# A fused two-block transformer on one core: weight splitting one tile further ahead among the gating steps of the second layer's FFN, and eighteen w_ada tiles moved into the first layer's FFN

## The chip, the core and the metric

The kernel runs on one core of a Trainium2 chip, as one program. The metric is the device time of one execution in microseconds (us). Five engines run their own instruction streams and meet at semaphores: TensorE (PE), VectorE (DVE), ScalarE (ACT), GpSimd (POOL) and SyncE (SP), which here only issues the DMAs.

## What is computed

A first block of two layers is followed by a second block of one layer. For this change, three pieces of the reference matter: the modulation vectors of each layer (`adaln_params`), the gated convolutional FFN, and the query projection of the second block's expert layer.

```python
def adaln_params(cvec, w_ada, b_ada):          # for c and for c_ctx
    m = jax.nn.silu(cvec) @ w_ada + b_ada      # w_ada: 1024 x 6144
    return jnp.split(m, 6, axis=-1)

def conv_ffn(h, w_up, conv_w, w_down):         # D_FF = 2816
    up = h @ w_up
    a, b = up[..., :D_FF], up[..., D_FF:]
    return (jax.nn.silu(dwconv3(a, conv_w)) * b) @ w_down

# trunk_layer, l = 0 (256 tokens and 256 context tokens) and l = 1 (256 tokens only):
x = x + gt1 * (mix @ w_out)
x = x + gt2 * conv_ffn(modulate(rmsnorm(x, g2), sh2, sc2), w_up, ffn_conv, w_down)

# second block: the same adaln, a mixer, then _peer, which begins with
q = (xb @ w_query).reshape(PEER_BLOCK, PEER_HEADS, 2, PEER_HALF)
```

## The kernel before

All weights stream from HBM in tiles of 128 x 1024 floats (512 KB), in one fixed order that `weight_tiles` writes down. Each tile lands in one of four buffers (`RAW`, `NRAW = 4`). SP issues the load of tile i when tile i-4 has been released, and it waits for that in the order of the list, so a late release holds back every later load.

A weight tile is not multiplied in one pass. ACT writes its rounded copy to `TH` ("high"), DVE or POOL writes the remainder to `TL` ("low"), and PE then runs three matmuls for each of the eight rows k (`mm3`: high x high, high x low, low x high). There are three such split buffers (`NSPLIT = 3`), so splitting tile j needs PE to be done with split tile j-3. A tile is released in `RAW` when its low part is written. `highs(n)` on ACT and `lows(n)` on DVE split, in order, every tile up to number n. `later(key, d)` is the split tile d places after `key`; `AHEAD = 2` is the usual distance.

The tiles of `w_ada` (48 for each of the three layers, 144 in all) are an exception: they are not split. PE multiplies them straight out of `RAW` with the silu of c in `SC`, into a bank of their own (`ada` on PE), and they occupy their `RAW` buffer until then. Every fourth one ends a group g: ACT copies the bank to `AROW`, and before the first tile of the next group PE turns that row into columns (`columns(g)`), to which DVE adds the bias. Groups in `ADA_TURNED` are turned at points written out by hand instead. `_ada_plan` says at which point of the program which w_ada tile stands: `("unit", l, u)` are points in attention, `("up", l, m)` and `("down", l, third, m)` points in the FFN, `("lstm", u)` and `("wq", m)` points in the second block.

The FFN of layer l has 22 gating steps m, in thirds of 8, 8 and 6. Step m projects tile `("wup", l, m)` (the part a), then tile `("wup", l, 22 + m)` (the part b). ACT copies a to `OC` times the middle tap (`conv_mid`), DVE adds the two outer taps, ACT applies silu, DVE multiplies by b ("gated"), ACT writes the rounded result to `MIDh` and DVE the remainder to `MIDl`. After each third come eight tiles `("wdn", l, third, i)` that multiply the mids, and DVE adds each result to X (`residual`). In the first layer a matmul row has 512 columns (48 matmuls of 256 columns for a tile), in the second 256 (24 matmuls for a tile). After the third third of the first layer, ACT squares each row of X for the next norm, and PE can go on only when that norm is done.

In the second layer's first third ACT also squares the context of the second block (`ctx`), and behind the first third PE sums it. Between the second layer's tiles wup 1 and wup 2, SP also loads a block of constants (`in_cs2`), for which it waits until the norm has read what lies there.

Where the splits stand among the gating steps of both layers, on ACT and on DVE:

```python
highs(later(("wup", l, mm_), 3 if mm_ == 0 else AHEAD))   # ACT, ahead of conv_mid
...
if mm_:
    highs(later(("wup", l, 22 + mm_), AHEAD))             # ACT, behind silu, ahead of MIDh
...
lows(later(("wup", l, mm_), 3 if mm_ == 0 else AHEAD))    # DVE, ahead of the taps
...
if mm_:
    lows(later(("wup", l, 22 + mm_), AHEAD))              # DVE, behind the taps, ahead of gated
```

## Time and profile before

| | us |
|---|---|
| median of three runs | 2350.66 (2347.52 to 2355.02) |
| the profiled execution, its own time | 2337.34 |
| its span, first to last instruction | 2335.6 |
| PE busy | 2172.3 (93%) |
| DVE busy | 1285.3 (55%) |
| ACT busy | 1086.5 (47%) |
| DMA, mean rate | 152 GB/s |
| mean granted clock of TensorE | 0.957 of full |

PE busy counts each matmul from its issue to its modelled end, and those overlap, so 93% does not mean that PE has little left to lose: a matmul of 256 columns has a duration of about 280 ns but the next may start 113 ns after it. The granted clock is 1 at 2.4 GHz and 0.5 at 1.2 GHz.

### The profile page before, as it was taken

The numbers are of one execution on the slowest core, as the hardware profiler recorded it, in microseconds if no ns is written. First come the engines' busy times: TensorE is split into PE (matmuls) and PEld (weight loads), VectorE is DVE, ScalarE is ACT, GpSimd is POOL, SyncE is SP. The second block draws the span as 40 slices with busy tenths as digits, with TensorE's granted clock in tenths as the row PEclk, the third lists the DMA queues.
The fourth block names the chain that finished last, engine by engine and source line by source line (L and its number), as shares of the span: only waits on it lengthen the run. The fifth ranks groups of instructions, "written<-read, shape, count | busy, mean of one in ns | idle before, by whom it ended". The sixth has DMA issues, their size and how long they took to land.

```text
span 2335.6 us, 44498 instructions
## 1 busy us (share of the span) xinstructions
PE 2172.3 (93%) x19132; PEld 2038.7 (87%) x19132; DVE 1285.3 (55%) x2517; ACT 1086.5 (47%) x1880; POOL 485.4 (21%) x230
## 2 busy tenths in 40 slices
PE   4989999999999888899878998899999999999998
PEld 3967889999999678888857888899999999999998
DVE  2253444343444465455546255559938898666665
ACT  3333343232235335344533344555567776655564
POOL 0201100000002110000211234128866665000000
PEclk8999989999998899999879999999999999999999
DMA  7224323434433245655323333465644444566654
GB/s 272 73 82 137 126 86 141 146 136 154 154 118 121 73 166 190 222 172 204 114 69 128 135 118 126 154 226 186 195 153 145 151 145 157 193 196 192 197 191 135
DMA packets 97284, 355.01 MB, mean 152 GB/s; under 512 B 10688, under 2 KB 11712, under 8 KB 96704
## 3 DMA queue, kind: packets, MB, share of 16 engines
q1 hardware_dynamic: 97088, 352.18, 44.8%
q8 instruction: 150, 2.46, 0.4%
q14 instruction: 46, 0.38, 0.0%
HBM read 351.09 MB, written 1.05 MB: 151 GB/s over the span
## 4 chain that ended last, share of the span: by engine, by line
PE 77%; DVE 8%; ACT 5%; issue 5%; DMA 4%; POOL 2%; SPq 0%; DVEq 0%; POOLq 0%; ACTq 0%
PE ps L79 72%; PE ps L84 4%; DVE TL L114 3%; ACT TH L158 3%; PE ps L107 1%; POOL TL L114 1%; DMA RAW<-in_wup 1%; DMA RAW<-in_wada 1%; DMA RAW<-in_wdn 1%; DVE l1oc L126 1%; POOL SM L114 1%; ACT SQ L155 1%; DMA RAW<-in_win 0%; ACT l1oc L155 0%; DMA RAW<-in_wq 0%
## 5 line engine op out<-in xcount | busy, mean ns | idle before, releaser
L158 ACT ACTIVATE TH<-RAW 128x1024 fp32r<-128x1024 f32 (+1 forms) x515 | 539.5, 1049 | 395.1 <-PE ps L79 155.8
L114 DVE TENSOR_TENSOR TL<-RAW,TH 128x1024 fp32r<-128x1024 f32 (+1 forms) x339 | 414.3, 1222 | 416.8 <-ACT TH L158 416.3
L114 POOL TENSOR_TENSOR TL<-RAW,TH 128x1024 fp32r<-128x1024 f32 x176 | 423.3, 2408 | 606.8 <-ACT TH L158 588.3
L79 PE MATMUL ps<-Hh,TL 128*128 128x256 f32 x1920 | 457.6, 291 | 52.5 <-POOL TL L114 19.0
L79 PE MATMUL ps<-Hh,TH 128*128 128x256 f32 x1920 | 444.8, 284 | 0.0
L79 PE MATMUL ps<-Hl,TH 128*128 128x256 f32 x1920 | 443.6, 284 | 0.0
L79 PEld LDWEIGHTS ps<-Hh,TL 128*128 128x128 f32 x1920 | 327.4, 195 | 84.8 <-issue 28.2
L79 PE MATMUL ps<-HXh,TL 128*128 128x256 f32 x1312 | 368.2, 285 | 17.4 <-DVE TL L114 12.0
L79 PE MATMUL ps<-HXh,TH 128*128 128x256 f32 x1312 | 361.8, 280 | 0.0
L79 PE MATMUL ps<-HXl,TH 128*128 128x256 f32 x1312 | 361.0, 279 | 0.0
L79 PE MATMUL ps<-W,TH 128*128 128x256 f32 x2048 | 348.2, 276 | 0.0
L79 PEld LDWEIGHTS ps<-Hh,TH 128*128 128x128 f32 x1920 | 327.8, 195 | 0.1
L79 PEld LDWEIGHTS ps<-Hl,TH 128*128 128x128 f32 x1920 | 327.7, 195 | 0.0
L79 PEld LDWEIGHTS ps<-W,TH 128*128 128x128 f32 x2048 | 308.6, 188 | 0.0
L79 PE MATMUL ps<-W,TL 128*128 128x256 f32 x1024 | 283.2, 277 | 1.5 <-DVE G L114 1.5
L79 PEld LDWEIGHTS ps<-HXh,TL 128*128 128x128 f32 x1312 | 248.2, 191 | 21.2 <-DVE TL L114 13.5
L79 PEld LDWEIGHTS ps<-HXh,TH 128*128 128x128 f32 x1312 | 248.4, 191 | 0.0
L79 PEld LDWEIGHTS ps<-HXl,TH 128*128 128x128 f32 x1312 | 247.4, 190 | 0.0
L79 PEld LDWEIGHTS ps<-W,TL 128*128 128x128 f32 x1024 | 192.3, 188 | 1.7 <-DVE G L114 1.7
L114 POOL TENSOR_TENSOR ACC<-SQ 128x512 f32<-128x512 f32 (+1 forms) x6 | 7.6, 1269 | 604.1 <-ACT SQ L155 604.1
L126 DVE SCALAR_TENSOR_TENSOR X<-ps,ADA,X 128x256 f32<-128x256 f32 x104 | 47.1, 480 | 136.3 <-PE ps L79 136.3
L155 ACT ACTIVATE W<-W,T 128x128 fp32r<-128x128 f32 x256 | 82.0, 391 | 64.6 <-DVE W L114 64.6
(323 smaller groups left out, 3070.2 us busy)
## 6 DMA issues: line engine op xcount, KB each, us to landing
RAW<-in_wada SPq DMA_DIRECT2D x144, 512.0 KB, 3.9
RAW<-in_ut SPq DMA_DIRECT2D x128, 512.0 KB, 3.5
RAW<-in_v SPq DMA_DIRECT2D x128, 512.0 KB, 3.5
RAW<-in_wup SPq DMA_DIRECT2D x88, 512.0 KB, 3.7
RAW<-in_win SPq DMA_DIRECT2D x74, 512.0 KB, 3.7
RAW<-in_wdn SPq DMA_DIRECT2D x32, 512.0 KB, 4.5
RAW<-in_wout SPq DMA_DIRECT2D x24, 512.0 KB, 3.6
RAW<-in_wq SPq DMA_DIRECT2D x16, 512.0 KB, 3.7
```

Source lines behind the costliest of these rows:

```text
L79: return self.e.matmul(out, lhs, rhs, start=first, stop=last, skip_group_check=skip)
L84: return self.e.matmul(out, lhs, rhs, start=first, stop=last, tile_position=at)
L107: return self.e.transpose(out, src, eye)
L114: return DRY if self.e is None else self.e.tensor_tensor(out, a, b, op)
L126: return self.e.scalar_tensor_tensor(out=out, in0=a, scalar=s, in1=b, op0=op0, op1=op1)
L155: return DRY if self.e is None else self.e.activation(out, a, fn, **kw)
L158: return DRY if self.e is None else self.e.activation(out, a, ACT.Copy, **kw)
```

## The change

1. In the second layer's FFN (l = 1), the splits among the gating steps run three tiles ahead instead of two, and they stand elsewhere: on ACT one behind `conv_mid` and one behind silu, on DVE one behind the taps and one behind the multiplication by b. The last of the eight wdn steps of the first and second thirds also splits three ahead.
2. Eighteen w_ada tiles move forward in the plan: eight leave the second layer's gating steps, two the lstm points and eight the wq points. Ten get a new point `"between"` (between a and b of the first layer's steps 12 to 21), eight stand at the wdn steps of the first layer's last third. All that follow shift along: the second layer's attention now holds tiles 0 to 9 of the third w_ada, for instance. Group 21, 23, 27 and 33 are now turned like the others.
3. SC gets the next layer's silu right behind the last tile of a w_ada on ACT, no longer ahead of the first tile of the next.
4. In the wdn steps of both layers DVE splits ahead of the residual, no longer behind it.

```diff
@@ weight_tiles
                 add(("wup", l, m), ins[f"wup{l}"][m])
+                ada("between", l, m)
                 add(("wup", l, 22 + m), ins[f"wup{l}"][22 + m])
...
         add(("wq", m), ins["wq2"][m])
-        ada("wq", m)
@@ _ada_plan
-    plan += [(("up", 0, m), 1) for m in range(8)]
-    plan += [(("down", 0, 0, m), 1) for m in range(8)]
-    plan += [(("up", 0, m), 1) for m in range(8, 16)]
-    plan += [(("down", 0, 1, m), 1) for m in range(8)]
-    plan += [(("up", 0, m), 1) for m in range(16, 22)]
+    for third in range(3):
+        for m in range(8 * third, min(8 * third + 8, 22)):
+            plan += [(("between", 0, m), 1)] * (m >= 12) + [(("up", 0, m), 1)]
+        plan += [(("down", 0, third, m), 1) for m in range(8)]
...
-    plan += [(("up", 1, m), 1) for m in range(8)]
...
-    plan += [(("lstm", u), 1) for u in range(6)]
-    plan += [(("wq", m), 1) for m in range(1, 16, 2)]
+    plan += [(("lstm", u), 1) for u in range(4)]
-ADA_TURNED = (3, 9, 11, 21, 23, 27, 33, 35)
+ADA_TURNED = (3, 9, 11, 35)
@@ scalar_program, ada
-                if i == 0 and b:
-                    act.wait_ge(P, *used("wada", b - 1, 47))
-                    act.act(SC, par(["c1", "c1", "c2"][b]), ACT.Silu).then_inc(*A.mark("sc", b))
...
+                if i == 47 and b < 2:
+                    act.act(SC, par(["c1", "c2"][b]), ACT.Silu).then_inc(*A.mark("sc", b + 1))
@@ scalar_program, gating steps
-                    highs(later(("wup", l, mm_), 3 if mm_ == 0 else AHEAD))
+                    if l == 0:
+                        highs(later(("wup", l, mm_), 3 if mm_ == 0 else AHEAD))
                     act.wait_ge(P, *used("wup", l, mm_))
...
                         .then_inc(*A.mark("conv_mid", l, mm_))
+                    if l:
+                        highs(later(("wup", l, mm_), 3))
+                    else:
+                        ada("between", l, mm_)
                     act.wait_ge(D, "conv", l, mm_)
                     act.act(o, o, ACT.Silu).then_inc(*A.mark("silu", l, mm_))
-                    if mm_:
+                    if l:
+                        highs(later(("wup", l, 22 + mm_), 3))
+                    elif mm_:
                         highs(later(("wup", l, 22 + mm_), AHEAD))
...
-                    highs(later(("wdn", l, third, i), AHEAD))
+                    highs(later(("wdn", l, third, i), 3 if l and third < 2 and i == 7 else AHEAD))
@@ vector_program, gating steps
                     conv_taps(("conv", l, mm_), o, ps("z", "wup", l, mm_)[:, 0:T], tap, len(strs))
-                    if mm_:
+                    ada("between", l, mm_)
+                    if l:
+                        lows(later(("wup", l, mm_), 3))
+                    elif mm_:
                         lows(later(("wup", l, 22 + mm_), AHEAD))
...
                     dve.tt(o, o, ps("z", "wup", l, 22 + mm_)[:, 0:T], ALU.mult).then_inc(*D.mark("gated", l, mm_))
+                    if l:
+                        lows(later(("wup", l, 22 + mm_), 3))
...
                 for i in range(8):
+                    lows(later(("wdn", l, third, i), AHEAD))
                     dve.wait_ge(P, *used("wdn", l, third, i))
                     residual(("res2", l, third, i), ps("z", "wdn", l, third, i), l, i, 5, strs)
-                    lows(later(("wdn", l, third, i), AHEAD))
+                    if l and third < 2 and i == 7:
+                        lows(later(("wdn", l, third, i), 3))
```

How the instructions stand now, at three places. ACT in the second layer's FFN, second third; `TH<-RAW` is a split, `l1oc<-ps` the copy of a, `l1oc<-l1oc` silu, `l1midh` the rounded mid. Before:

```order
L158 ACTIVATE TH<-RAW 128x1024
L158 ACTIVATE l1oc0<-ps0,P 128x256
L155 ACTIVATE l1oc0<-l1oc0 128x256
L158 ACTIVATE TH<-RAW 128x1024
L158 ACTIVATE l1midh<-l1oc0 128x256
```

And in the changed kernel:

```order
L158 ACTIVATE l1oc0<-ps3,P 128x256
L158 ACTIVATE TH<-RAW 128x1024
L155 ACTIVATE l1oc0<-l1oc0 128x256
L158 ACTIVATE TH<-RAW 128x1024
L158 ACTIVATE l1midh<-l1oc0 128x256
```

The split that stood ahead of the copy of a now stands behind it; both splits are of a tile one further on. DVE in the same steps; `TL<-RAW,TH` is the low part of a split, the pair of `l1oc<-ps,P,l1oc` the taps, `l1oc<-l1oc,ps` the multiplication by b. Before:

```order
L114 TENSOR_TENSOR TL<-RAW,TH 128x1024
L126 SCALAR_TENSOR_TENSOR l1oc0<-ps0,P,l1oc0 128x255 x2
L114 TENSOR_TENSOR TL<-RAW,TH 128x1024
L114 TENSOR_TENSOR l1oc0<-l1oc0,ps1 128x256
L114 TENSOR_TENSOR l1midl<-l1oc0,l1midh 128x256
```

And in the changed kernel:

```order
L126 SCALAR_TENSOR_TENSOR l1oc0<-ps3,P,l1oc0 128x255 x2
L114 TENSOR_TENSOR TL<-RAW,TH 128x1024
L114 TENSOR_TENSOR l1oc0<-l1oc0,ps4 128x256
L114 TENSOR_TENSOR TL<-RAW,TH 128x1024
L114 TENSOR_TENSOR l1midl<-l1oc0,l1midh 128x256
```

Each low part has moved behind one step of the gating. SP at the end of the first layer's FFN, where `in_wdn0 128x768` are the eight tiles of its last third and `in_win1` the next layer's first tiles. Before:

```order
L2521 DMA RAW<-in_wup0 128x1024 x2
L2521 DMA RAW<-in_wada1 128x1024
L2521 DMA RAW<-in_wup0 128x1024 x2
L2521 DMA RAW<-in_wada1 128x1024
L2521 DMA RAW<-in_wdn0 128x768 x8
L2521 DMA RAW<-in_win1 128x1024 x7
```

And in the changed kernel, whose rows between the first and the last of these wdn tiles repeat the same pair:

```order
L2527 DMA RAW<-in_wup0 128x1024
L2527 DMA RAW<-in_wada1 128x1024
L2527 DMA RAW<-in_wup0 128x1024
L2527 DMA RAW<-in_wada1 128x1024
L2527 DMA RAW<-in_wdn0 128x768
L2527 DMA RAW<-in_wada1 128x1024
L2527 DMA RAW<-in_wdn0 128x768
L2527 DMA RAW<-in_wada1 128x1024
L2527 DMA RAW<-in_win1 128x1024 x7
```

A w_ada tile now stands behind every wup tile of steps 12 to 21 and behind each of the last eight wdn tiles.

## Rows read from the trace of the kernel before

**Rows 1.** ACT's timeline, one gating step: start, us, operation, [idle before <-releaser].
```profile
1002.23 0.45 ACT L158 ACTIVATE l1oc<-ps,P 128x256 f32<-128x256 f32 x1
1004.53 0.42 ACT L155 ACTIVATE l1oc<-l1oc 128x256 f32<-128x256 f32 x1 [1.85 <-DVE l1oc L126]
1004.85 1.05 ACT L158 ACTIVATE TH<-RAW 128x1024 fp32r<-128x1024 f32 x1
1007.52 0.42 ACT L158 ACTIVATE l1midh<-l1oc 128x256 fp32r<-128x256 f32 x1 [1.62 <-DVE l1oc L114]
1008.79 0.46 ACT L158 ACTIVATE l1oc<-ps,P 128x256 f32<-128x256 f32 x1
```

**Rows 2.** Timeline of DVE in the same step.
```profile
1003.50 1.00 DVE L126 SCALAR_TENSOR_TENSOR l1oc<-ps,P,l1oc 128x255 f32<-128x255 f32 x2
1005.93 1.22 DVE L114 TENSOR_TENSOR TL<-RAW,TH 128x1024 fp32r<-128x1024 f32 x1 [1.44 <-ACT TH L158]
1007.07 0.41 DVE L114 TENSOR_TENSOR l1oc<-l1oc,ps 128x256 f32<-128x256 f32 x1
1007.97 0.43 DVE L114 TENSOR_TENSOR l1midl<-l1oc,l1midh 128x256 fp32r<-128x256 f32 x1 [0.48 <-ACT l1midh L158]
```

**Rows 3.** Waits of PE, 890 to 1111 us: us in total, times, longest.
```profile
PE ps L79 <- DVE TL L114: 14.0, 21, 2.9
```

**Rows 4.** Timeline of DVE, first layer's wdn steps: residuals of successive tiles.
```profile
439.89 0.88 DVE L126 SCALAR_TENSOR_TENSOR X<-ps,ADA,X 128x256 f32<-128x256 f32 x2 [4.20 <-PE ps L79]
446.09 0.88 DVE L126 SCALAR_TENSOR_TENSOR X<-ps,ADA,X 128x256 f32<-128x256 f32 x2 [4.20 <-PE ps L79]
452.62 0.88 DVE L126 SCALAR_TENSOR_TENSOR X<-ps,ADA,X 128x256 f32<-128x256 f32 x2 [4.44 <-PE ps L79]
...
685.36 0.88 DVE L126 SCALAR_TENSOR_TENSOR X<-ps,ADA,X 128x256 f32<-128x256 f32 x2 [2.48 <-PE ps L79]
689.44 0.88 DVE L126 SCALAR_TENSOR_TENSOR X<-ps,ADA,X 128x256 f32<-128x256 f32 x2 [2.34 <-PE ps L79]
```

**Rows 5.** Timeline of DVE, the first layer's last residual.
```profile
713.92 0.88 DVE L126 SCALAR_TENSOR_TENSOR X<-ps,ADA,X 128x256 f32<-128x256 f32 x2 [3.21 <-PE ps L79]
```

**Rows 6.** Timeline of PE at the borders of the second layer's thirds.
```profile
903.67 0.58 PE L79 MATMUL ps<-Hh,TL 128*128 128x256 f32 x1 [2.87 <-DVE TL L114]
...
949.83 0.60 PE L79 MATMUL ps<-P,AROW 128*128 128x8 f32 x2 [4.25 <-ACT AROW L158]
...
986.58 0.39 PE L79 MATMUL ps<-Hh,TL 128*128 128x256 f32 x1
...
1069.11 0.39 PE L79 MATMUL ps<-Hh,TL 128*128 128x256 f32 x1 [1.33 <-DVE TL L114]
...
1110.24 0.38 PE L79 MATMUL ps<-l1midh,TL 128*128 128x256 f32 x1 [1.38 <-ACT l1midh L158]
```

**Rows 7.** Timeline of DVE, first residual of the first and of the second third.
```profile
958.82 0.48 DVE L126 SCALAR_TENSOR_TENSOR X<-ps,ADA,X 128x256 f32<-128x256 f32 x1 [4.80 <-PE ps L79]
...
1041.74 0.48 DVE L126 SCALAR_TENSOR_TENSOR X<-ps,ADA,X 128x256 f32<-128x256 f32 x1 [0.48 <-PE ps L79]
```

**Rows 8.** SP's issue of the constants; page part 6: KB, us to landing.
```profile
893.32 0.33 SPq L2514 DMA_DIRECT2D C<-in_cs  x1
...
RAW<-in_wup SPq DMA_DIRECT2D x88, 512.0 KB, 3.7
...
C<-in_cs SPq DMA_DIRECT2D x1, 1216.0 KB, 5.3
```

**Rows 9.** Windows: us, busy by engine; then PEclk, DMA share, GB/s.
```profile
950.00:960.00 10.00, 10.00 (x64) 9.63 (x65) 1.57 (x5) 1.24 (x3) 0.71 (x1) 0.59 0.01 2
1050.00:1060.00 10.00, 9.81 (x109) 8.94 (x112) 3.79 (x5) 3.35 (x4) 0.00 (x0) 1.00 0.83 282
```

**Rows 10.** Timeline of PE, query projection: first w_ada tile, and the keys behind it.
```profile
1503.96 0.62 PE L84 MATMUL ps<-RAW,SM 128*2 128x128 f32 x16
...
1550.35 1.13 PE L79 MATMUL ps<-RAW,G 128*128 128x128 f32 x8
```

More of the change, by code:

```diff
@@ L860, in tensor_program @@
                          ks=MIX_ORDER, midway=lambda: head_spread(1))
-            columns(12 * l + 9)
+            if l == 0:
+                columns(9)
             for i in range(2, 8):
@@ L880, in tensor_program @@
                 if third == 0:
-                    columns(12 * l + 11)
                     if l:
                         norm(("ctx",), 256)
-                if (l, third) == (1, 2):
-                    columns(27)
+                    else:
+                        columns(11)
                 for i in range(8):
@@ L1054, in tensor_program @@
         ring[0] = Ring(range(7), bank_of, bank_until)
-        columns(33)
+        columns(35)
         gate_tile(28)
@@ L1127, in tensor_program @@
         ring[0] = rest
-        columns(35)
         up(0, 30)
@@ L1413, in scalar_program @@
                 for mm_ in ms:
-                    highs(later(("wup", l, mm_), 3 if mm_ == 0 else AHEAD))
+                    if l == 0:
+                        highs(later(("wup", l, mm_), 3 if mm_ == 0 else AHEAD))
                     act.wait_ge(P, *used("wup", l, mm_))
@@ L1947, in vector_program @@
             mix_low(7)
-            columns(12 * l + 9)
+            if l == 0:
+                columns(9)
             scales(("m2", l), l, f"n2g{l}", 4, 1)
@@ L1961, in vector_program @@
                 for mm_ in ms:
-                    lows(later(("wup", l, mm_), 3 if mm_ == 0 else AHEAD))
+                    if l == 0:
+                        lows(later(("wup", l, mm_), 3 if mm_ == 0 else AHEAD))
                     def tap(i):
@@ L1969, in vector_program @@
                     conv_taps(("conv", l, mm_), o, ps("z", "wup", l, mm_)[:, 0:T], tap, len(strs))
-                    if mm_:
+                    ada("between", l, mm_)
+                    if l:
+                        lows(later(("wup", l, mm_), 3))
+                    elif mm_:
                         lows(later(("wup", l, 22 + mm_), AHEAD))
@@ L1979, in vector_program @@
                 if third == 0:
-                    columns(12 * l + 11)
                     if l:
                         above(("ctx",), ROOT[1][:, 2:4], 1024 * EPS)
-                if (l, third) == (1, 2):
-                    columns(27)
+                    else:
+                        columns(11)
                 if third == 2:
@@ L2249, in vector_program @@
         branch_low(1)
-        columns(33)
+        columns(35)
         scales(("m2", 2), 2, "n2g2", 4, 1)
@@ L2279, in vector_program @@
             lows(min(later(("wq", c), 3), at_tile["wq", 15]))
-            ada("wq", c)
         for half in range(2):
             lows(at_tile["keys", half] + AHEAD)
-        columns(35)
         def sixteen(key, v, i, src, rest):
```

4 lines of the change are left out of this document (1 added, 3 removed).

## The prediction

> **What bounds the kernel now.** I read the page first: PE is busy in nearly every slice, ACT and DVE about half of the time. So the question at each place is whether PE runs without a gap, since there a w_ada tile costs its full PE time, or waits, since there it may cost nothing or more than its own time. I then went through the timelines of PE, ACT, DVE and SP stage by stage.
>
> First layer's FFN. PE has no gaps there. Successive residuals in the wdn steps show it: with 48 matmuls and a w_ada tile 6.20 us, with a turn of a group 6.53, and in the last third, with 36 matmuls and no w_ada, 4.08 [rows 4]. So a matmul of 256 columns takes 4.08/36 = 0.1133 us, a full tile of 48 takes 5.44, a w_ada tile 0.76 and a turn 0.33. A tile of the second layer (24 matmuls) is 2.72.
>
> Second layer's FFN. Two tiles would take PE 5.44 us, but a gating step of the second third takes 1008.79 - 1002.23 = 6.56 [rows 1]. The reader should see that neither ACT nor DVE is full and that they take turns: ACT idles 1.85 for the taps and 1.62 for the multiplication, and DVE idles 1.44 for the high part [rows 1, 2]. The step is one chain of split high (1.05), split low (1.22), taps (1.00), silu (0.42), high (1.05), low (1.22), gated (0.41), mid (0.42): 6.8, less small overlaps, which is the 6.56. PE waits for the low parts that hang in it, 14.0 us in 21 waits [rows 3].
>
> Borders. Three long stretches stand between the chain's steps: the wait for tile wup 2 (2.87), whose load stands behind the constants; the turn of group 23 (4.25 for AROW), which ACT reaches only behind its last gating step; then the second block's silu for SC, which holds back the first w_ada tile of wdn 0 and the loads behind it [rows 6, 7]. The granted clock fell to 0.59 behind them [rows 9].
>
> **The change, part by part.**
>
> *Gating steps of the second layer.* The new order breaks the chain. With U the end of PE's tile a: ACT copies a (0.45), splits (1.05), silu at about U+1.6; DVE does the taps until U+1.6, a low part until U+2.8. Tile b ends at U+2.72; ACT splits until U+3.9, DVE gates until U+3.3, ACT writes the mid until U+4.3, DVE the low part and the mid's until U+5.5. That is within PE's 5.44 per step, with a low part done 2.6 to 3.1 us before PE wants it. DVE's own work is 1.00 + 2 x 1.22 + 0.41 + 0.43 = 4.3 [rows 2], so it is not the bound. I take 2.75 for a tile.
>
> The second third, from its first matmul at 986.58 to the end of the first wdn tile at 1041.74, is 55.2 us [rows 6, 7] for 17 tiles. After: 17 x 2.75 + 1.0 = 47.8. The 1.0 is a wait at the mids' last row: ACT now splits wdn 2 ahead of the last mid, and that load is issued only when wdn 0 is split. Gain 7.4. The last third, from 1069.11 to 1110.6 (three matmuls behind 1110.24), is 41.5 [rows 6]; after, 12 x 2.75 + 2.04 + 1.0 = 36.0; gain 5.5. Bounds of both together: 4 if a step stays at 6.1, halfway to the old one, and 15 with no wait at all.
>
> *The first third.* Eight w_ada tiles leave, but the constants still block SP until 893.32. They need 5.3 us to land and wup 2 follows directly: about 898.6 plus 1.9 for one tile at 282 GB/s, so 900.5, plus 2.4 for the split: PE begins it at 902.9, against 903.67 [rows 6, 8, 9]. So this wait stays.
>
> The Trainium skill, page "DMA: Bandwidth & Descriptors", section "Queues, rings and completion order", says that each DMA engine takes descriptors of a ring in order; by it no earlier start than this one is to be had. Did the two share the engines evenly instead, wup 2 would be split about 1.3 us sooner, and the sum would be 1.3 better.
>
> Then 12 tiles are 33.0, and I add 2.0 for the clock: the window behind the longer stop lost 0.41 of 10 us [rows 9], and I take half of 4.1 for a shorter one (bounds 0 and 4.1). PE is at the end of the third at 937.9. The turn of group 23 and the silu are gone from here (both now lie in the first layer or in attention), but PE still sums the context's squares, the last of which follows the split of wdn 2 and the last mid on ACT: 3.0 us. The first wdn tile then ends at 937.9 + 3.0 + 2.72 + 2.0 (clock) = 945.6, against 958.8 [rows 7]. Gain 13.2; bounds 9 (both clock losses in full) and 18.
>
> *The wdn steps with w_ada.* 27.8 us from 958.82 to 986.58, and 27.4 from 1041.74 to 1069.11 [rows 6, 7]. PE alone would need 7 x 2.72 + 8 x 0.76 + 2 x 0.33 = 25.8, but each step loads two tiles, 1.05 MB, at the 282 GB/s seen there [rows 9]: 3.7 a step, 26.8 in all. Gains 0.9 and 0.6. Bounds: -1 and +3.
>
> The same page, section "Bandwidth", has about 358 GB/s for one core from HBM. By that figure a step's loads would take 2.9 us and the steps would be PE's 25.8, some 2.6 us more gained; the trace's 282 decides, and I stay with it.
>
> *Query projection.* From the first w_ada tile at 1503.96 to the keys at 1550.35 is 46.4 us [rows 10] for 13 tiles and eight w_ada tiles. Splits already run three ahead there. After: 13 x 2.75 + 0.5 (the first split waits for PE) + 0.3 (last copy) = 36.6. Gain 9.8; bounds 6 (the w_ada tiles alone, 8 x 0.76) and 11. *The lstm points:* PE has no gap there; 2 x 0.76 = 1.5.
>
> *What the first layer pays.* 18 x 0.76 = 13.7, and four more turns at 0.33 = 1.3: 15.0, all of it in a stretch where PE has no gap. I cost the loads at nothing: a step of 12.4 us now carries four tiles, and the longest path (load 3.7, split 2.3) has about 11 us. If a load came more than 5 us late, it would show as a PE wait in each of ten steps.
>
> The end of that FFN costs more. DVE now splits ahead of the residual, and at the last wdn tile this split is of the next layer's second tile, whose load waits for the last but one w_ada tile. From there: 3.7 + 1.05 + 1.22 + 0.1 = 6.1, whereas the residual could start at 4.08 (in before it started as PE ended, 713.92 [rows 5]). The norm behind it starts 2.0 later; the last w_ada tile (0.76) lies in that wait. Net 1.3; bounds -0.8 and 3.
>
> *Attention of the second layer:* the numbering has moved, so that the end of a group and the start of the next now meet in one unit; PE waits for ACT's AROW there. 1.0, bounds 0 and 2. The other edits (SC earlier, residual later in other steps) have nobody waiting: the banks are a ring of seven and X is read next a norm later.
>
> **Sum.** Gains 13.2 + 0.9 + 7.4 + 0.6 + 5.5 + 9.8 + 1.5 = 38.9. Costs 15.0 + 1.3 + 1.0 = 17.3. Net 21.6. Against the profiled execution: 2337.34 - 21.6 = 2315.7. That execution was 13 us faster than the median of the three timed runs, so for the median I subtract the same: 2350.66 - 21.6 = 2329.
>
> **Rivals.**
> 1. *The chain only half breaks.* ACT now waits for b before the mid, and DVE has a low part ahead of the mid's. If each semaphore hop cost 0.3 more than I took, DVE's 4.3 plus ten hops would pass 5.44 and a step would stay near 6.1. Gain in the three thirds some 10 us less: 2339. Against it: after a releaser's end the hops seen are 0.05 or so [rows 1, 2].
> 2. *Everything fits.* No stop at the borders, no clock loss, wdn steps at PE's pace: +9 on the gain, 2320. Against it: the constants and the context's norm are untouched.
> 3. *No change.* The first layer's FFN is not as patient as I say (late loads of half a us in the 18 places, the norm 3 us late) and the chain half breaks: net under 7, 2344 to 2357.
> 4. *Slower.* A w_ada tile between a and b holds its RAW buffer until PE has used it, and SP stops in order behind it, so tile b of the next step comes late. The price is how much load plus split exceeds the 11 us available. It decides from 4 us of PE wait in each of ten steps, 40 us against the 21.6 won: 2369. For it: the order of loads really does stop at each w_ada tile. Against it: 3.7 to land, and the steps with one w_ada tile per pair show no PE wait at all.
>
> **How the numbers follow.** A measurement of this kernel can tell about 0.3% (7 us) from no change. Forecast, 2323 to 2335: 0.62. Half-broken chain, about 2339: 0.14. Everything fits, about 2320: 0.14. No change: 0.06. Slower: 0.04. From the first three, faster 0.90. The range goes from 2319 to 2343: it leaves out the last two cases and the far end of the third.
>
> **What would show it.** After: gating steps of the second layer 5.5 us apart, PE's waits for TL there under 4 us in total, its first wdn residual some 13 us earlier relative to the norm ahead of it; wup 2 still waited for; keys 36.6 us behind the first three query tiles; first layer's FFN 15 us longer and the residual of its last tile late by 2. Wrong would be: steps above 6 us, new PE waits in the first layer's last third, or a query projection that still waits for splits.

## The result, and the profile after

The changed kernel takes 2327.32 us, median of 9 executions (2320.37 to 2334.49). Its ratio to the kernel before (2350.66, of nine executions) is 0.9905, with a 95% interval of 0.9882 to 0.9928. Forecast were 2329 us, 2319 to 2343. The total was right; several terms of the sum were not, and they nearly cancel, in part by luck.

The page of the profile, for the changed kernel (own time 2327.22 us):

```profile
span 2325.4 us, 44521 instructions
...
PE 2177.1 (94%) x19132; PEld 2046.2 (88%) x19132; DVE 1288.2 (55%) x2517; ACT 1089.6 (47%) x1880; POOL 485.6 (21%) x230
```

Busy times have hardly moved, and the two profiled spans differ by only 10.2 us where the medians differ by 23.3. So the comparison has to go by stages. As marks I took starts of DVE instructions, which sit at the same places in all kernels: the first gating step of the first layer's FFN, each first and last residual, the first MAX8 behind the query projection, and the first and last step of the expert down stage. For the second layer's FFN these are DVE's residuals in the changed kernel; the first row ends the output projection, then first and last of each group of wdn steps:

```profile
884.17 0.48 DVE L126 SCALAR_TENSOR_TENSOR X<-ps,ADA,X 128x256 f32<-128x256 f32 x1 [1.10 <-PE ps L79]
...
945.47 0.48 DVE L126 SCALAR_TENSOR_TENSOR X<-ps,ADA,X 128x256 f32<-128x256 f32 x1 [2.58 <-PE ps L79]
...
976.92 0.48 DVE L126 SCALAR_TENSOR_TENSOR X<-ps,ADA,X 128x256 f32<-128x256 f32 x1
...
1023.08 0.48 DVE L126 SCALAR_TENSOR_TENSOR X<-ps,ADA,X 128x256 f32<-128x256 f32 x1 [0.48 <-PE ps L79]
...
1053.34 0.48 DVE L126 SCALAR_TENSOR_TENSOR X<-ps,ADA,X 128x256 f32<-128x256 f32 x1
...
1086.55 0.48 DVE L126 SCALAR_TENSOR_TENSOR X<-ps,ADA,X 128x256 f32<-128x256 f32 x1
...
1108.60 0.48 DVE L126 SCALAR_TENSOR_TENSOR X<-ps,ADA,X 128x256 f32<-128x256 f32 x1
```

Against 958.82 and 1041.74 of before [rows 7], the stages are (us; the column "residual first" is the third experiment below, which differs from the changed kernel only in item 4 of the change):

| stage | before | changed | difference | forecast | residual first |
|---|---|---|---|---|---|
| first layer's FFN, first gating step to last residual | 379.0 | 394.3 | +15.3 | +17.0 | 393.0 |
| norm and attention of the second layer | 147.4 | 140.3 | -7.0 | +0.3 | 144.8 |
| output projection | 18.4 | 17.1 | -1.3 | 0 | 17.6 |
| norm and first third | 79.1 | 61.3 | -17.8 | -13.2 | 62.0 |
| wdn 0, first to last residual | 27.3 | 31.4 | +4.1 | -0.9 | 27.3 |
| second third | 55.6 | 46.2 | -9.4 | -7.4 | 48.8 |
| wdn 1 | 27.2 | 30.3 | +3.0 | -0.6 | 26.2 |
| last third | 42.3 | 33.2 | -9.1 | -5.5 | 36.0 |
| last wdn steps | 14.2 | 22.0 | +7.9 | 0 | 14.3 |
| second block, to its output projection | 342.8 | 342.1 | -0.7 | -1.5 | 340.4 |
| output projection | 19.1 | 19.0 | -0.1 | 0 | 19.8 |
| norm and query projection | 70.7 | 61.5 | -9.2 | -9.8 | 59.8 |
| expert up stage (same code) | 413.0 | 416.0 | +3.0 | 0 | 416.4 |
| expert down stage (same code) | 353.9 | 367.5 | +13.6 | 0 | 367.5 |

Differences are taken before rounding. The forecast's 15.0 for the tiles plus 2.0 for the late residual stand in the first row; the rest of its 1.3 and the 1.0 of attention in the second. Up to the down stage the changed kernel is 23.8 us ahead (1971.0 against 1947.2), close to the 23.3 between the medians; 2.5 of it lie ahead of the first row, where the code is the same in both. The down stage then takes 13.6 back in this pair of executions; that it belongs to the execution and not to the kernel is shown below.

One gating step of the second third, in the timeline of ACT and DVE of the changed kernel, to be read beside [rows 1, 2]:

```profile
988.67 0.47 ACT L158 ACTIVATE l1oc<-ps,P 128x256 f32<-128x256 f32 x1 [1.40 <-PE ps L79]
989.04 1.05 ACT L158 ACTIVATE TH<-RAW 128x1024 fp32r<-128x1024 f32 x1
989.18 1.00 DVE L126 SCALAR_TENSOR_TENSOR l1oc<-ps,P,l1oc 128x255 f32<-128x255 f32 x2 [0.62 <-ACT l1oc L158]
990.12 1.23 DVE L114 TENSOR_TENSOR TL<-RAW,TH 128x1024 fp32r<-128x1024 f32 x1
990.21 0.42 ACT L155 ACTIVATE l1oc<-l1oc 128x256 f32<-128x256 f32 x1
991.55 1.06 ACT L158 ACTIVATE TH<-RAW 128x1024 fp32r<-128x1024 f32 x1 [0.93 <-PE ps L79]
991.57 0.42 DVE L114 TENSOR_TENSOR l1oc<-l1oc,ps 128x256 f32<-128x256 f32 x1 [0.21 <-PE ps L79]
992.52 0.40 ACT L158 ACTIVATE l1midh<-l1oc 128x256 fp32r<-128x256 f32 x1
992.65 1.22 DVE L114 TENSOR_TENSOR TL<-RAW,TH 128x1024 fp32r<-128x1024 f32 x1 [0.66 <-ACT TH L158]
993.79 0.42 DVE L114 TENSOR_TENSOR l1midl<-l1oc,l1midh 128x256 fp32r<-128x256 f32 x1
```

ACT now waits for PE (1.40 and 0.93) where it waited for DVE (1.85, 1.62). DVE waits 0.21 for PE, and for ACT only 0.62 and 0.66 where it was 1.44; no wait of ACT for DVE is left in the step. The multiplication by b starts 5.65 us after that of the step before (985.91, 991.57), against 6.56 from step to step before; in the first and last thirds most steps are 5.44 apart, PE's 48 matmuls exactly. The chain broke as forecast.

What had not been forecast is in the last wdn steps. Timeline of ACT, POOL and DVE there, changed kernel:

```profile
1090.76 0.83 ACT L158 ACTIVATE TH<-RAW 128x768 fp32r<-128x768 f32 x1
1091.00 1.29 POOL L114 TENSOR_TENSOR ACC<-SQ 128x512 f32<-128x512 f32 x1 [147.32 <-ACT SQ L155]
1091.62 1.48 DVE L114 TENSOR_TENSOR TL<-RAW,TH 128x768 fp32r<-128x768 f32 x1 [1.62 <-ACT TH L158]
1093.03 0.47 DVE L126 SCALAR_TENSOR_TENSOR X<-ps,ADA,X 128x256 f32<-128x256 f32 x1
...
1093.54 0.42 ACT L155 ACTIVATE SQ<-X 128x256 f32<-128x256 f32 x1 [1.94 <-DVE X L126]
1093.86 0.49 ACT L155 ACTIVATE SQ<-X,P 128x256 f32<-128x256 f32 x1
1094.26 0.83 ACT L158 ACTIVATE TH<-RAW 128x768 fp32r<-128x768 f32 x1
```

This is a ring: ACT's high part (0.86 until the low part starts), DVE's low part (1.41 until the residual starts), the residual (0.51 until ACT squares), two squares (0.72 until the next high part), together 3.50 us from 1090.76 to 1094.26. PE needs 2.04 us for such a step (18 matmuls). ACT waits 1.94 for DVE and DVE 1.62 for ACT, in turn, just as in the gating steps of before. Item 4 of the change (low part ahead of the residual) had tied a new chain while item 1 untied the old one. That this is the cause is tested below ("residual first", "squares later").

### The profile page after: what moved, and what is told of

Read it like the earlier page. It is cut to its first block, busy times and chain, and to the rows that moved or that the text cites. A ratio compares the mean times of both kernels' runs of the same rounds, so it can differ in the third digit from the quotient of the medians.

```text
span 2325.4 us, 44521 instructions
## 1 busy us (share of the span) xinstructions
PE 2177.1 (94%) x19132; PEld 2046.2 (88%) x19132; DVE 1288.2 (55%) x2517; ACT 1089.6 (47%) x1880; POOL 485.6 (21%) x230
## 4 chain that ended last, share of the span: by engine, by line
PE 79%; DVE 6%; issue 5%; ACT 4%; DMA 3%; POOL 2%; SPq 0%; DVEq 0%; POOLq 0%; ACTq 0%
PE ps L79 74%; PE ps L84 4%; DVE TL L114 2%; ACT TH L158 2%; POOL TL L114 1%; DMA RAW<-in_wdn 1%; PE ps L107 1%; DMA RAW<-in_wada 1%; ACT SQ L155 1%; POOL SM L114 1%; DMA RAW<-in_wup 1%; DMA RAW<-in_win 0%; ACT Hh L158 0%; DVE ps L114 0%; DVE l1st L132 0%
## 5 line engine op out<-in xcount | busy, mean ns | idle before, releaser
L79 PEld LDWEIGHTS ps<-Hh,TL 128*128 128x128 f32 x1920 | 325.9, 194 | 74.7 <-issue 29.9
L79 PE MATMUL ps<-W,TH 128*128 128x256 f32 x2048 | 361.9, 281 | 0.0
L84 PE MATMUL ps<-RAW,SM 128*2 128x128 f32 x2304 | 94.5, 289 | 14.9 <-DMA RAW<-in_wada 14.9
```

Of the source, the lines that this page charges most:

```text
L79: return self.e.matmul(out, lhs, rhs, start=first, stop=last, skip_group_check=skip)
L84: return self.e.matmul(out, lhs, rhs, start=first, stop=last, tile_position=at)
```

## The experiments

The table gives them in the stages that they were made for; each is told below.

| kernel | first layer's FFN | norm, first third | wdn 0 | second third | wdn 1 | last third | last wdn | query projection | ratio to before |
|---|---|---|---|---|---|---|---|---|---|
| before | 379.0 | 79.1 | 27.3 | 55.6 | 27.2 | 42.3 | 14.2 | 70.7 | 1 |
| changed | 394.3 | 61.3 | 31.4 | 46.2 | 30.3 | 33.2 | 22.0 | 61.5 | 0.9905 |
| splits only | 379.7 | 79.6 | 28.6 | 49.8 | 28.6 | 36.9 | 14.2 | 70.0 | 0.9923 |
| w_ada only | 393.3 | 74.5 | 27.0 | 56.1 | 26.1 | 41.2 | 14.3 | 61.6 | 0.9957 |
| residual first | 393.0 | 62.0 | 27.3 | 48.8 | 26.2 | 36.0 | 14.3 | 59.8 | 0.9856 |
| low part first, alone | 379.3 | 82.1 | 29.8 | 54.2 | 27.2 | 39.9 | 22.0 | 70.8 | 1.0038 |
| squares later | 393.8 | 63.3 | 28.4 | 46.4 | 30.6 | 34.8 | 14.6 | 60.9 | 0.9819 |
| eight back | 387.4 | 60.8 | 25.8 | 49.1 | 29.9 | 37.0 | 14.3 | 71.6 | 0.9863 |
| constants later | 392.9 | 60.4 | 27.1 | 49.3 | 27.4 | 35.8 | 14.8 | 60.1 | 0.9838 |

**Splits only.** The kernel before with item 1 alone:

```diff
-                    highs(later(("wup", l, mm_), 3 if mm_ == 0 else AHEAD))
+                    if l == 0:
+                        highs(later(("wup", l, mm_), 3 if mm_ == 0 else AHEAD))
...                  # behind conv_mid, and behind silu; DVE's low parts likewise
+                    if l:
+                        highs(later(("wup", l, mm_), 3))
```

> The kernel before with the new places of the splits in the second layer's FFN alone (change 1); the w_ada plan and the residual's place are those of before. My theory (the gating chain was the bound there, and splitting three ahead breaks it whatever the w_ada plan is): second third from the first residual of its wdn ahead to its own, 55.6 us before, becomes 46.2, last third 42.3 becomes 33.2, as in the changed kernel, and with the residual ahead of the low part the wdn steps stay at 27.3, 27.3 and 14.1. In the first third a w_ada tile still follows every tile b, and a split three ahead has to wait until PE has used it: I expect no gain there (79.1, 73 to 84). Total 15 to 22 us less than before, ratio 0.991 to 0.994. Rival (the gain needs the w_ada tiles gone too, since the loads are the bound): second and last third stay above 50 and 38.

Measured: ratio 0.9923 (0.989 to 0.9955), median 2332.57. Second and last third fall by 5.8 and 5.4, and the first third not at all. The forecast of 46.2 and 33.2 for the two was missed by 3.6 and 3.7, and 49.8 stands just at the rival's bound of 50, so the stage times alone don't decide. The steps do: in this kernel DVE's multiplications by b are 5.65 us apart in the second third and 5.44 in the last, as in the changed kernel, while the two kernels that keep the old splits ("w_ada only" and "low part first, alone") stay at 6.56. So the chain theory holds for the steps, and the rival (loads as the bound) falls; the 3.6 and 3.7 belong to item 4, which moves the marks (below). The median is 17.3 us under that of before, inside the 15 to 22 forecast, but the stages account for only 8.0 of it up to the down stage, so the total was not met for the reason given; its ten times spread from 2322 to 2345 us, and which down stage each of them had is not known. Why the first third gains nothing is in its waits, 886 to 950 us (us in total, times, longest):

```profile
ACT TH L158 <- DMA RAW<-in_wup: 14.6, 6, 5.3
...
PE ps L79 <- ACT AROW L158: 6.4, 1, 6.4
```

ACT, asked for a tile that lies beyond a w_ada tile, stands in front of a load that SP can't issue until PE has used that tile. With this order of splits and four buffers, the split three ahead and a w_ada tile in every step don't go together.

**w_ada only.** The changed kernel's plan (items 2 and 3) on the splits and residuals of before:

```diff
+            plan += [(("between", 0, m), 1)] * (m >= 12) + [(("up", 0, m), 1)]
+        plan += [(("down", 0, third, m), 1) for m in range(8)]
...
-    plan += [(("up", 1, m), 1) for m in range(8)]
...
-    plan += [(("wq", m), 1) for m in range(1, 16, 2)]
```

> The kernel before with the w_ada tiles moved (changes 2 and 3) and nothing else: splits and residuals stand as before. My theory (each tile moved out of a stretch with waits gives back less than its PE time, since the chain of the gating step is longer than PE's work): first layer's FFN 379.0 becomes 394 (15 more; without the late last residual), the second layer's norm and attention 147.4 becomes 140 to 147 (what it lost in the changed kernel was low clock behind a shorter stop, 8.6 us at a granted share below 1 of which the clock halves PE), first third with its norm 79.1 becomes 68 to 75, second and last third unchanged (55.6, 42.3), query projection 70.7 becomes 61.4. Net 5 to 15 less, ratio 0.994 to 0.998. Rival (the gain of the first third is all of the splits): first third 77 or more, net 0.

Measured: ratio 0.9957 (0.9926 to 0.9988), median 2338.22. First layer +14.3, first third -4.6, query projection -9.1. The eight tiles that left the first third have 8 x 0.76 = 6.1 us of PE time, and 4.6 came back. It did not come from the steady steps: the gating step, still the old chain, is spaced 6.87 us without w_ada (DVE multiplies by b at 905.42, 912.29, 919.16) and was 6.86 to 6.88 in most steps with it. The seven steps together are 2.3 shorter, 1.9 of that in the first one, which holds the wait for wup 2, and from the last step to the first residual it takes 7.0 for 10.1, where the turn of group 23 has left as well. So the first third gains 0 by the splits, 4.6 by the move, and 17.1 by both: neither part is worth much there without the other.

**Residual first.** The changed kernel with item 4 undone:

```diff
                 for i in range(8):
-                    lows(later(("wdn", l, third, i), AHEAD))
                     dve.wait_ge(P, *used("wdn", l, third, i))
                     residual(("res2", l, third, i), ps("z", "wdn", l, third, i), l, i, 5, strs)
+                    lows(later(("wdn", l, third, i), AHEAD))
```

> The changed kernel with DVE's residual ahead of its low part in the wdn steps again (change 4 undone), all else as changed. My theory (the low part ahead of the residual ties high, low, residual, two squares and the next high into one chain of about 3.5 us per step where PE needs 2.04): the second layer's last eight wdn steps 22.1 us become 14 (steps 2.04), wdn of its first and second third 31.4 and 30.2 become 27 to 28, the first layer's last residual comes 2 us earlier; in all 12 to 17 us less than the changed kernel, ratio to before 0.983 to 0.986. Rival A (the wdn steps are longer because the gating steps ran ahead of the loads, which now have to be made up for): 31.4 and 30.2 stay, only the last wdn steps change, 8 us less, ratio 0.987. Rival B (order has no part, as the prediction had it): nothing changes, 0.9905.

Measured: ratio 0.9856 (0.981 to 0.9903), median 2318.23, so 9 us below the changed kernel. The last wdn steps are back at PE's pace, 2.04 us apart. Timeline of DVE:

```profile
1093.47 0.48 DVE L126 SCALAR_TENSOR_TENSOR X<-ps,ADA,X 128x256 f32<-128x256 f32 x1 [0.48 <-PE ps L79]
...
1095.51 0.48 DVE L126 SCALAR_TENSOR_TENSOR X<-ps,ADA,X 128x256 f32<-128x256 f32 x1 [0.49 <-PE ps L79]
```

wdn 0 and wdn 1 fall by 4.1 and 4.0. But the second and last thirds behind them are 2.7 and 2.8 longer than in the changed kernel. With the low part first, a residual stands late in its step, and the next third's tiles are further advanced when the last of them starts: most of the 4.1 is a mark that moved, not time. What is left, 1.5 and 1.2 us, is no more than what these stages differ by between executions of one kernel (wdn 1 of the kernel before took 27.2 and 29.4), so rival A (loads to be made up for) is neither needed nor excluded there. Over the whole FFN of the second layer, from the last residual of the output projection to the last of all, item 4 costs 224.43 - 214.68 = 9.8 us, of which 7.8 in the last steps, where rival B falls. I had expected 12 to 17 in all; the 2 us at the first layer's end were wrong too (below).

**Low part first, alone.** The reverse edit on the kernel before:

```diff
                 for i in range(8):
+                    lows(later(("wdn", l, third, i), AHEAD))
                     dve.wait_ge(P, *used("wdn", l, third, i))
                     residual(("res2", l, third, i), ps("z", "wdn", l, third, i), l, i, 5, strs)
-                    lows(later(("wdn", l, third, i), AHEAD))
```

> The kernel before with DVE's low part ahead of the residual in the wdn steps of both layers (change 4 alone). My theory: the second layer's last wdn steps 14.1 become 20 to 22, its wdn 0 and wdn 1 27.3 each become 28 to 31, the first layer's last residual 0 to 2 us later; 8 to 15 slower in all, ratio 1.003 to 1.006. Rival (the low part ahead of the residual costs only together with the splits three ahead): last wdn steps 14 to 16, ratio 1.000.

Measured: ratio 1.0038 (1.001 to 1.0066), median 2358.71, slower by 9 us. Last wdn steps 22.0, and over the second layer's FFN 255.2 against 245.7 us, 9.5 more (7.7 against the 247.5 of the repeat). wdn 1 stays at 27.2, where 28 to 31 were forecast. In the last wdn steps item 4 costs the same with and without the rest of the change, 7.8 and 7.9; the rival (only together with the splits) falls.

**Squares later.** The changed kernel, item 4 kept; in the second layer's last wdn steps ACT squares the row before:

```diff
                     if third == 2:
-                        act.wait_ge(D, "res2", l, 2, i)
                         if l == 0:
+                            act.wait_ge(D, "res2", l, 2, i)
                             square(("n1", 1), i, X[:, i, :])
-                        else:
-                            square(("final",), i, X[:, i, 0:256], par("finalg", i, i + 1))
+                        for j in [[], [i - 1] if i else [], [6, 7]][l * (1 + (i == 7))]:
+                            act.wait_ge(D, "res2", l, 2, j)
+                            square(("final",), j, X[:, j, 0:256], par("finalg", j, j + 1))
```

> The changed kernel, with the low part still ahead of the residual in all wdn steps, but in the second layer's last eight wdn steps ACT squares row i-1 behind the high part where it squared row i (the last two rows come together at the end). My theory (the 3.5 us step is the chain high part, low part, residual, two squares, next high part, and no engine is full): this cuts the squares out of the chain without touching DVE's order, so the seven steps from first to last residual, 22.0 in the changed kernel, become 14 to 16. Rival (the low part ahead of the residual loads DVE itself, whose low part takes up to 1.48 us beside POOL's sum, or the tiles come late): they stay at 20 or more. Everything ahead of these steps as in the changed kernel. Total 6 to 8 less than the changed kernel, ratio to before 0.987 to 0.988.

Measured: last wdn steps 14.6 us, though DVE's order is the changed one. So it was the ring, not DVE's load and not the tiles. Timeline of ACT and DVE:

```profile
1094.63 0.48 DVE L126 SCALAR_TENSOR_TENSOR X<-ps,ADA,X 128x256 f32<-128x256 f32 x1
1094.69 0.85 ACT L158 ACTIVATE TH<-RAW 128x768 fp32r<-128x768 f32 x1 [0.49 <-PE ps L79]
1095.44 0.40 ACT L155 ACTIVATE SQ<-X 128x256 f32<-128x256 f32 x1
1095.57 0.96 DVE L114 TENSOR_TENSOR TL<-RAW,TH 128x768 fp32r<-128x768 f32 x1 [0.46 <-ACT TH L158]
```

The high part now waits for PE and no longer for the squares. The ratio is 0.9819 (0.9765 to 0.9874) from only four executions; in the profile the second layer's FFN is 6.4 us shorter than the changed kernel's (218.0 against 224.4) and 3.4 longer than that of "residual first", so I don't take the ratio as a sign that it is the better of the two. Up to the down stage the profile is only 1.6 us ahead of the changed kernel's, for 6 to 8 forecast: it starts the first layer's FFN 2.0 later, and its second block takes 1.8 more, both in code that is the same.

**Eight back.** "Residual first", with the eight w_ada tiles of the first layer's last wdn steps returned to the query projection:

```diff
-        plan += [(("down", 0, third, m), 1) for m in range(8)]
+        plan += [(("down", 0, third, m), 1) for m in range(8) if third < 2]
...
+    plan += [(("wq", m), 1) for m in range(1, 16, 2)]
```

> The residual-first version of the changed kernel, with the eight w_ada tiles of the first layer's last wdn steps given back to the query projection; the group that ends there is turned by hand again as before. By the prediction's prices: first layer's last wdn steps from first to last residual 34.5 become 28.5, the query projection with its norm 59.8 becomes 69 to 71, everything else unchanged, so net 3 to 4 us slower than the residual-first version, ratio 0.987. Rival (a w_ada tile costs the same everywhere, its 0.76 us of PE): the query projection gets only 6 slower and the net is 0.

Measured: the first layer's last wdn steps 34.5 become 28.6 (-5.9 for 6.1 forecast), the query projection 59.8 becomes 71.6 (+11.8). The 71.6 lies above the 69 to 71 forecast, so the net of the two stages is 5.9 where 3 to 4 were forecast; the rival (the same price everywhere) falls. The prices differ by place: where PE has no gap a tile costs its 0.76, in the query projection it costs about 1.5 (11.8 / 8). PE's waits show half of the other 5.7: from 1450 us to the keys it waits 3.5 us for low parts here (2.70 of it at 1480.23) and 0.4 with the residual first. The remaining 2.6 is not divided; the granted clock read 0.83 from 1480 to 1490 us. Up to the down stage this kernel is 5.7 us behind (1943.7 against 1938.0), within it 3.7 in wdn 1. There PE waits 3.1 us in all for low parts and for AROW (1.87 the longest), where it waits 0.6 with the residual first; since wdn 1 also differs by 2.2 us between the two profiles of the kernel before, I can't say how much belongs to the edit. The ratio, 0.9863 (0.9804 to 0.9922), can't tell it from "residual first".

**Constants later.** "Residual first", with the constants' load four gating steps later:

```diff
-            if key == ("wup", 1, 2):
+            if key == ("wup", 1, 6):
```

> The residual-first version of the changed kernel, with the load of the constants issued four gating steps later (ahead of tile wup 6 where it stood ahead of wup 2). My theory (the load of 1216 KB, 5.3 us, stands ahead of wup 2 just when no tile is in stock behind the norm): PE's waits for TL in the first two steps of the second layer's FFN, 0.7 and 1.4 us, go or shrink below 0.5 in sum, the stretch from the last residual of wout to the first of wdn, 62.0 us, becomes 59 to 60.5, and at step 6 the load hides behind tiles in stock. 2 us less in all, ratio 0.985. Rival (four buffers are too few to hide 5.3 us wherever it stands): a wait of 1 to 3 us appears at steps 6 to 8 instead, net 0 or slower. Rival (the waits there are those of the splits behind the norm, not of the load): they stay.

Measured: ratio 0.9838 (0.9792 to 0.9883), median 2308.88 (2298.38 to 2318.04). Up to the down stage it is the shortest of all (1933.5 us, 1936.5 in the repeat, for 1947.2 in the changed kernel), and its interval lies below that of the changed kernel but for their ends (0.9883, 0.9882): it is the version I would keep. PE's timeline from 893 to 940 us shows one wait for a split where "residual first" had two (0.73 and 1.44, at 904.71 and 909.16). The one for wup 2 is gone; the sum did not fall below the 0.5 forecast:

```profile
903.33 0.39 PE L79 MATMUL ps<-Hh,TL 128*128 128x256 f32 x1 [0.73 <-DVE TL L114]
```

No wait comes in its place at step 6. Norm and first third take 60.4 us for 62.0 (60.9 in the repeat below): the load hides once tiles are in stock. The gain is 1.1 to 1.6 us in this stage, the theory's lower end. Over the whole second layer's FFN it is not to be seen in the first profile (214.8 us for 214.7) and 1.8 in the repeat (212.9), and the times alone don't separate the two kernels.

**Repeats.** Three kernels were profiled once more, unchanged, for the down stage.

> The kernel before, unchanged, profiled once more. The expert down stage (from the first expansion of gates to the last addition to the output), the same code in all kernels, took 353.9 us in the executions profiled of the kernel before and of the one with the constants later, and 367.5 in all six others. If the shorter value belongs to an execution and not to a kernel, a repeat mostly shows 367.5 and a total near 2350; if it belongs to the kernel, it shows 353.9 again and about 2337.

> The changed kernel, unchanged, profiled once more. Its down stage took 367.5 us. If the value belongs to an execution it may be either; in both cases the stages of the second layer's FFN repeat within 2 us: 61.3, 31.4, 46.2, 30.3, 33.2, 22.0.

> The version with the residual first and the constants later, unchanged, profiled once more. Down stage 353.9 the first time; 367.5 mostly, if the value belongs to an execution. The stretch with the norm and the first third repeats at 60.4, 1 to 2 us below the 62.0 of the version with the constants ahead of wup 2.

Measured: before 2348.55 us, down stage 367.5; changed 2309.16, down stage 353.9; constants later 2302.92, down stage 353.9. The value belongs to the execution: the kernel before has shown both, and so has the changed one. In twelve profiled executions it was four times 353.9 and eight times 367.5 or 367.6, with nothing between. Up to the down stage the repeats take 1968.5 and 1942.8 us, 25.8 apart, for 23.8 in the first pair. The stages of the second layer's FFN of the changed kernel repeat at 62.8, 31.1, 46.3, 29.5, 34.1 and 22.1; over that FFN the changed kernel is 21.3 us shorter in the first pair and 21.6 in the repeats.

## Why the prediction was right, and where not

**The gating chain: right.** Steps of 5.44 and 5.65 us for the 5.5 forecast. "Residual first" shows the terms without item 4: second third -6.8 for -7.4 forecast, last third -6.3 for -5.5, wdn 0 and 1 together -1.0 for -1.5. The two experiments with one part alone show that the gain needs the eight w_ada tiles gone in the first third, and not in the others.

**First third: the chain right, one wait misread and the clock's term too large.** -17.1 in "residual first" for -13.2 forecast, inside the bounds of 9 to 18. The timeline of PE, changed kernel, shows what is left of the 2.87 us wait [rows 6]:

```profile
902.90 0.39 PE L79 MATMUL ps<-Hh,TL 128*128 128x256 f32 x1 [0.66 <-DVE TL L114]
...
906.83 0.38 PE L79 MATMUL ps<-Hh,TL 128*128 128x256 f32 x1 [0.92 <-DVE TL L114]
```

I had written "So this wait stays". The first row is the second part of wup 1, the second row wup 2, the first tile behind the constants: its wait is 0.92. The forecast had the constants alone in its way, with wup 2 following directly. In the kernel before it did not follow directly. Timelines of SP and PE:

```profile
893.32 0.33 SPq L2514 DMA_DIRECT2D C<-in_cs  x1
897.29 0.80 SPq L2521 DMA_DIRECT2D RAW<-in_wup  x2
...
896.61 0.62 PE L84 MATMUL ps<-RAW,SM 128*2 128x128 f32 x16
```

SP issued wup 2 only 4.0 us behind the constants, when PE had used the w_ada tile in the buffer that it needed. In the changed kernel the four buffers hold four wup tiles there, and SP's next issue follows at once:

```profile
897.82 0.33 SPq L2520 DMA_DIRECT2D C<-in_cs  x1
898.19 25.59 SPq L2527 DMA_DIRECT2D RAW<-in_wup  x12
```

The constants themselves are issued 7.0 us behind PE's restart in both. Counted from that restart, wup 2 starts 16.0 us later (890.84 to 906.83) where it was 17.3 before (886.35 to 903.67), a gain of 1.3 for 0.8 forecast. The larger miss is the clock. The forecast charged 2.0 for a lowered clock twice, once behind wup 2 (in 937.9) and once at the border (in 945.6). Neither came: from 906.83 PE runs 288 matmuls without a wait in 32.9 us, the 33.0 of the forecast without its 2.0, and between 940 and 950 us the granted clock is 1.00. The 4.0 and the 0.5 are nearly all of the 4.6 by which the changed kernel's -17.8 goes beyond the forecast.

**"Residual later in other steps ... nobody waiting": wrong.** This is the step that failed. I checked who reads X next (a norm later) and forgot that in the last wdn steps ACT's squares read it at once, with the next high part queued behind them. It was forecast at 0 and costs 7.8 to 7.9 us there and 9.5 to 9.8 in the layer (7.7 against the repeat of the kernel before): with it (changed, low part first alone) the last steps take 22.0, without it 14.2 to 14.8, and with it but the squares moved 14.6.

**The first layer: right.** 18 tiles and four turns forecast at 15.0; +14.3 with w_ada alone, +14.0 with the residual first. **Its end: wrong by 1.3.** The last residual does come 1.2 us later with item 4, but PE's restart behind the norm doesn't: it is at 735.52 us in the changed kernel and at 735.68 with the residual first, 403.1 and 404.2 us behind the first gating step. What the norm waits for is PE's own sum of the squares, 32 matmuls behind the last w_ada tile. With the residual first, ACT's last square ends at 726.06, yet PE is at this sum until 729.49. In the changed kernel the last square ends at 728.24, while PE is still at the sum without a pause, and the sum ends at 729.35: the late residual is hidden there, so the forecast's 1.3 has no place. That the sum took longer with the residual first lies in the clock. Windows of the changed kernel and of "residual first" (us, PE busy and number of matmuls, granted clock, DMA share, GB/s):

```profile
727.00:728.00 1.00, 1.00 (x11) 1.00 0.78 274
728.00:729.00 1.00, 1.00 (x11) 1.00 0.51 205
```

```profile
727.00:728.00 1.00, 1.00 (x10) 0.84 0.87 348
728.00:729.00 1.00, 1.00 (x6) 0.50 0.03 12
```

The edit is not what lowered the clock: with the constants later, also with the residual first, PE restarts 403.3 us behind the first gating step.

**Attention of the second layer: wrong sign.** Forecast +1.0 for a wait for AROW. The wait came, and one for the squares shrank. PE in the changed kernel:

```profile
824.97 0.39 PE L79 MATMUL ps<-P,AROW 128*128 128x8 f32 x2 [1.04 <-ACT AROW L158]
...
842.47 0.58 PE L79 MATMUL ps<-P,SQ 128*128 128x2 f32 x4 [1.54 <-ACT SQ L155]
```

and in the kernel before:

```profile
833.75 0.58 PE L79 MATMUL ps<-P,SQ 128*128 128x2 f32 x4 [3.03 <-ACT SQ L155]
```

In the eight profiled executions with the new plan this stage takes 140.3 to 144.8 us, in the four with the old one 145.6 to 147.4, on average 142.4 and 146.3. So the -7.0 of the first pair overstates what the plan gives; about 4 is what the averages show. Within each group the granted clock varies. The same 8 us of the program, 72 us behind PE's restart, in windows of the kernel before, the changed kernel, and its repeat (us, PE busy and number of matmuls, granted clock, DMA share, GB/s):

```profile
796.80:804.80 8.00, 6.92 (x29) 0.57 0.00 0
```

```profile
807.50:815.50 8.00, 5.96 (x40) 1.00 0.13 35
```

```profile
807.50:815.50 8.00, 7.31 (x38) 0.79 0.12 23
```

How the shortening divides between the waits and the clock stays open.

**Query projection: right.** -9.2 for -9.8. From the first matmul of its fourth tile (1487.09) to the keys (1524.67) are 37.6 us, for 36.6 forecast. The 1.5 of the two lstm tiles can't be read off: the stage that holds them takes 340.0 to 343.9 us over the twelve profiled executions, 342.8 and 342.1 in the first pair.

**A slip beside the sum.** The forecast puts PE's pace in the two groups of wdn steps at "some 2.6 us more gained". From its own numbers it is (27.8 - 25.8) + (27.4 - 25.8) - 1.5 = 2.1; no term of the sum uses it.

**The offset between profile and median: right, without a reason at the time.** The forecast took 13 us off because the profiled execution of before was that much below its median. It was one with the short down stage, 13.6 us. That both medians are of executions with the long one is likely but not shown: of the changed kernel's nine times none is below 2320 us, where its repeat with the short stage took 2309.

So the total was right with some luck. Item 4 cost 9.8 that was not foreseen. Against it, the first third came out 3.9 better than forecast (by "residual first"), because a wait was misread and a clock loss did not come, and attention 7.3 better, of which the averages support about 4. What remains, 2.5 ahead of the first layer's FFN in one direction and 3.0 in the expert up stage in the other, is code that is the same.

Of the signs named ahead, "PE's waits for TL there under 4 us in total" depends on what is counted. The windows 895 to 1086 us, the stretch of [rows 3], and 1086 to 1111, the last wdn steps, show in the changed kernel:

```profile
PE ps L79 <- DVE TL L114: 6.4, 6, 1.7
...
PE ps L79 <- DVE TL L114: 3.9, 4, 1.2
```

Against the 14.0 of before this is 6.4, so the sign was missed; 2.9 of it (0.66, 0.92 and 1.29) stand at wup tiles, the rest in wdn 0 and wdn 1. The 3.9 are the ring. With the residual first the waits for TL from 870 to 1110 sum to 4.0 us.

## What to carry to other kernels

When an engine's instruction is moved ahead of another, the question is not only who reads the result of the delayed one last, but who reads it first, and what is queued behind that reader: in the last wdn steps a ring of high part, low part, residual, squares took the place of the ring that the change had opened. Two edits that each remove half of an obstacle should be costed together, since here one gave 0, the other 4.6 and both 17.1 us in the same third. And before two profiled executions are compared by their spans, look at a long stage whose code is the same in both.

## What the runs showed of the hardware

The same stream of matmuls runs at two paces while the granted clock reads 1.00. Windows of 20 us in the down stage (us, PE busy and number of matmuls, clock, DMA share, GB/s), kernel before, first profile and repeat:

```profile
2050.00:2070.00 20.00, 20.00 (x178) 1.00 0.59 188
```

```profile
2050.00:2070.00 20.00, 20.00 (x172) 1.00 0.53 187
```

and the changed kernel, first profile and repeat:

```profile
2050.00:2070.00 20.00, 20.00 (x172) 1.00 0.58 184
```

```profile
2050.00:2070.00 20.00, 20.00 (x179) 1.00 0.59 194
```

The windows also count matmuls that reach over their edges. Exact are the starts of DVE's low parts there, one for 24 matmuls: 2.72 us apart in the kernel before (2056.74, 2059.46) and 2.83 in the changed one (2058.68, 2061.51). So 0.113 or 0.118 us a matmul of 256 columns, 4% apart, held through a whole stage of 354 or 367 us. The durations of ACT's and DVE's splits there are the same (1.06 and 1.23 us) in both. The second third of the gating steps shows the slower pace too: 5.65 us for 48 matmuls against 5.44 in the thirds beside it, in the same execution. The Trainium skill ("TensorE: Matmul & The Clock Gate", section "Wait — 56ns, not 53.3ns?") gives as the spacing of back-to-back matmuls at the higher clock level the columns divided by 2.4 GHz plus about 2.5 ns; for 256 columns that is, as an estimate from the page's figure, 109 ns. Both paces seen here are longer. What chooses between them I can't say; no experiment was aimed at it.

DVE's low part of 768 columns takes 0.96 us alone (1088.65 in the changed kernel) and 1.48 when it starts while POOL sums squares (1091.62, POOL from 1091.00 for 1.29). The Trainium skill ("SBUF — State Buffer", section "SBUF: two separate sides") has DVE operations with two SBUF inputs and those of POOL that read SBUF share a pair of ports, which one holds for its whole instruction while the other waits. By it the low part would end at 1092.29 + 0.96 = 1093.25; it ended at 1093.10, so the rows agree to 0.15 us. It lengthens the ring above by 0.5 us in the four steps in which POOL sums: they are 3.48 to 3.51 us, and the step ahead of them, with the low part at 0.96, was 2.97 (1086.55 to 1089.52).
